# Mixture of experts: a third slot for expert weights, thirty blocks written out

## What is computed

```python
def expert_block(args):
    xb, e = args
    h = jax.nn.silu(xb @ w_gate[e]) * (xb @ w_up[e])
    return h @ w_down[e]

y_rows = lax.map(expert_block, (x_rows, block_e)).reshape(n_rows, d)
y = jax.ops.segment_sum(y_rows * row_gate[:, None], row_tok, num_segments=t + 1)[:t]
```

## Time and profile before

| | us |
|---|---|
| median of 3 runs | 4931.76 (4929.23 to 4942.64) |
| the profiled execution | 4922.4 |
| its span, first to last instruction | 4920.6 |
| experts of layer 0 / layer 1 within it | about 3115 to 3650 / 4291 to 4860 |
| TensorE busy | 3960.5 |
| VectorE / ScalarE / GpSimd busy | 1605.2 / 624.0 / 520.8 |
| moved by DMA | 708.19 MB, mean 144 GB/s |

### The profile page before, as it was taken

How to read it: one execution, slowest core, us unless ns; L and a number is a source line. 1 busy time by engine, 2 the same in 40 slices (tenths; PEclk the granted TensorE clock), 3 DMA queues, 4 the chain that set the end, 5 groups by cost and what they waited for, 6 DMA issues and landing times. The chain is left out here.

```text
span 4920.6 us, 53676 instructions
## 1 busy us (share of the span) xinstructions
PE 3960.5 (80%) x21959; PEld 2392.9 (49%) x21959; DVE 1605.2 (33%) x2927; ACT 624.0 (13%) x1247; POOL 520.8 (11%) x439
## 2 busy tenths in 40 slices
PE   4989978999898869998997548677757978587774
PEld 2578843444447734443476424344435756344442
DVE  6657733401384630002313651200021133310003
ACT  2211111000231220000111000000011022100000
POOL 1122310000101210001002311000010023100001
PEclk9999989999899989999997778799978997699997
DMA  3221215621220012221220011899972200499995
GB/s 121 69 74 50 105 47 189 204 81 60 61 69 10 2 67 83 69 90 47 83 77 1 0 60 58 332 401 402 405 278 80 74 1 1 170 394 399 401 408 234
DMA packets 243084, 708.19 MB, mean 144 GB/s; under 512 B 22140, under 2 KB 117812, under 8 KB 192084
## 3 DMA queue, kind: packets, MB, share of 16 engines
q1 hardware_dynamic: 223172, 662.03, 36.1%
q10 hardware_dynamic: 15120, 26.76, 1.5%
q0 software_dynamic: 4608, 16.78, 0.9%
HBM read 668.28 MB, written 37.24 MB: 143 GB/s over the span
## 5 line engine op out<-in xcount | busy, mean ns | idle before, releaser
L86 PE MATMUL ffn_in_ps<-ut,ffn_in_ring 128*128 128x512 f32 x1408 | 613.2, 596 | 25.5 <-DMA ffn_in_ring<-in_ffn_w_in 25.5
L2862 PE MATMUL experts_pg<-moe_wg,experts_xt 128*64 128x256 f32 x4224 | 515.1, 406 | 125.6 <-DMA moe_wg<-in_moe_w_up 104.9
L2862 PEld LDWEIGHTS experts_pg<-moe_wg,experts_xt 128*64 128x64 f32 x4224 | 326.3, 147 | 297.4 <-issue 145.5
L86 PEld LDWEIGHTS ffn_in_ps<-ut,ffn_in_ring 128*128 128x128 f32 x1408 | 266.6, 190 | 362.5 <-issue 336.2
L465 PE MATMUL ffn_out_y<-ffn_out_ring,ffn_h 128*128 128x512 f32 x704 | 308.4, 600 | 19.7 <-DMA ffn_out_ring<-in_ffn_w_out 19.7
L2877 PE MATMUL experts_py<-moe_wd,experts_ht 128*64 128x512 f32 x1056 | 266.6, 650 | 41.7 <-DVE experts_ht L2929 24.2
L86 PE MATMUL att_proj_ps<-att_proj_ring,ut 128*128 128x512 f32 x576 | 250.4, 598 | 16.3 <-DMA att_proj_ring<-in_attn_w_qkv 16.3
L2927 DVE TENSOR_TENSOR experts_h<-experts_hs,experts_pg 128x256 f32<-128x256 f32 x66 | 27.8, 422 | 628.1 <-ACT experts_hs L2896 628.1
L465 PEld LDWEIGHTS ffn_out_y<-ffn_out_ring,ffn_h 128*128 128x128 f32 x704 | 135.2, 193 | 190.1 <-issue 168.7
L86 PEld LDWEIGHTS att_proj_ps<-att_proj_ring,ut 128*128 128x128 f32 x576 | 177.7, 309 | 88.7 <-DMA att_proj_ring<-in_attn_w_qkv 16.7
L573 DVE TENSOR_TENSOR ffn_h<-ffn_in_act_out,ffn_in_ps 128x512 f32<-128x512 f32 x44 | 30.3, 688 | 531.9 <-ACT ffn_in_act_out L560 531.9
(11 more groups left out here) (632 smaller groups left out, 5478.1 us busy)
## 6 DMA issues: line engine op xcount, KB each, us to landing
moe_wg<-in_moe_w_gate SPq DMA_DIRECT2D x66, 2048.0 KB, 20.0
moe_wg<-in_moe_w_up SPq DMA_DIRECT2D x66, 2048.0 KB, 24.4
moe_wd<-in_moe_w_down SPq DMA_DIRECT2D x66, 2048.0 KB, 25.1
ffn_in_ring<-in_ffn_w_in SPq DMA_DIRECT2D x44, 1024.0 KB, 7.6
ffn_in_ada_ring<-in_ada_w SPq DMA_DIRECT2D x28, 1024.0 KB, 7.3
ffn_out_ring<-in_ffn_w_out SPq DMA_DIRECT2D x22, 1024.0 KB, 4.8
ssd_proj_ring<-in_ssd_w_in SPq DMA_DIRECT2D x20, 1024.0 KB, 5.3
att_proj_ring<-in_attn_w_qkv SPq DMA_DIRECT2D x9, 2048.0 KB, 7.9
```

The costliest lines, as they stand in the source:

```text
L86: last = nc.tensor.matmul(out, lhsT, rhs, start=(i == 0), stop=(i == len(pairs) - 1))
L2862: last = nc.tensor.matmul(pg[ch * SLOTS:(ch + 1) * SLOTS, b, side, 0:HH], xt[:, b, kk % MQ, kk // MQ, :], wg[:, b, side, kk, ch * HH:(ch + ...
```

## The change

There are three weight slots in place of two. The weights' buffers and semaphores move into a Stage of their own around routing and experts, so that its end adds a barrier; the outer one keeps its own. During routing three experts are loaded in place of two. In the experts' stage blocks 0 to 29 (`PLAIN`) are written out on every engine, with slot n mod 3 and the expert as a constant; blocks 30 and on run in the loop with slots 0 and 1. `load` on SP is split into `load_rows` and `load_weights`; the waits for rows are as before, those for the weights of a written-out block n are for gu_made and y_made of n - 2, that is block n - 3. All else is the same code, indented further.

```diff
+WSLOTS, PLAIN = 3, FIRST - 2
-        wg, wd = outer.sb("wg", [P, 2, 2, DK, HID]), outer.sb("wd", [P, 2, HK, D])
-        gu_in, d_in = ([outer.sem(f"{n}{b}") for b in range(2)] for n in ("gu_in", "d_in"))
+        weights = Stage(nc, f"moe_w{l}")
+        wg, wd = weights.sb("wg", [P, WSLOTS, 2, DK, HID]), weights.sb("wd", [P, WSLOTS, HK, D])
+        gu_in, d_in = ([weights.sem(f"{n}{b}") for b in range(WSLOTS)] for n in ("gu_in", "d_in"))
...
+        with weights:
...
-                    for b in range(2):
+                        for b in range(WSLOTS):
...
+                        def load_rows(i, b, first=False):
+                            r0 = sp.value_load(info[0:1, bass.ds(i + B, 1)], min_val=0, max_val=ASSIGN + SLOTS)
+                            if not first:
+                                sp.wait_ge(s["xt_made"], i - 1)
+                            for half in range(2):
+                                sp.dma_start(xg[half * SLOTS:(half + 1) * SLOTS, b, :],
+                                             x_rows[bass.ds(r0, SLOTS), half * HALF:(half + 1) * HALF]).then_inc(x_in[b], 16)
+
+                        def load_weights(e, w, before):
+                            sp.wait_ge(s["gu_made"], before)
+                            load_gate_up(sp, e, w)
+                            sp.wait_ge(s["y_made"], before)
+                            load_down(sp, e, w)
+
+                        for n in range(PLAIN):
+                            load_rows(n, n % 2, n < 2)
+                            if n >= WSLOTS:
+                                load_weights(slice(n, n + 1), n % WSLOTS, n - WSLOTS + 1)
+                        with sp.Fori(PLAIN // 2, more + 1) as it:
+                            for b in range(2):
+                                i = 2 * it + b
+                                e = sp.value_load(info[0:1, bass.ds(i, 1)], min_val=0, max_val=E - 1)
+                                load_rows(i, b)
+                                load_weights(bass.ds(e, 1), b, i - 1)
...
-                        pe.wait_ge(gu_in[b], 32 * it + 32)
+                            pe.wait_ge(gu_in[w], 32 * used + 32)
...
-                        pe.wait_ge(d_in[b], 16 * it + 16)
+                            pe.wait_ge(d_in[w], 16 * used + 16)
...
-                    one(0, 0, 0, True)
-
-                    one(1, 1, 0, True)
-                    with pe.Fori(1, more + 1) as it:
-                        for b in range(2):
-                            one(2 * it + b, b, it)
+                        for n in range(PLAIN):
+                            one(n, n % 2, n // 2, n % WSLOTS, n // WSLOTS, n < 2)
+                        with pe.Fori(PLAIN // 2, more + 1) as it:
+                            for b in range(2):
+                                one(2 * it + b, b, it, b, it - PLAIN // 2 + PLAIN // WSLOTS)
```

498 lines of the change are left out of this document (240 added, 258 removed).

## The result

The changed kernel takes 4966.84 us (median of 6 runs, 4954.52 to 4969.68), the kernel before 4934.08 beside it (6 runs, 4929.23 to 4942.64). The ratio is 1.0059, with a 95% interval of 1.0042 to 1.0075: some 29 us slower. The profiled execution of after took 4969.25 us (span 4967.3), against 4922.4 of before. The latter is a quick one: it lies under all six of these runs of before, and of the 58 runs of before beside the experiments only three lie under it. So where a stretch of its trace is set against that of another kernel, the difference is on the large side, by some 15 us over both layers: 4922.4 against medians of 4934 to 4940.

A forecast was written before the change was run, and what follows sets the result against it. TensorE bounds most of the kernel, DMA transfers the two layers' expert stretches. Per layer -16.9 + 7.5 + 10.8 + 1.2 = +2.6 us, +5 in both; from the 4931.8 median, 4937 was predicted, range 4917 to 4964.

The forecast's parts named there:

- The likeliest case, no change: Whole kernel: time between 4917 and 4947, within 0.3% (15 us) of before; chance 0.65.
- the 0.23 for slower: Whole kernel: chance 0.23 of a time over 4947, slower by more than 0.3%.
- Part 2: Experts' stage: the first loop load waits for block 1's transposes, so the DMA-bound stretch begins later: +7.5 us a layer.
- part 3: Routing: the third expert's load runs into the token scatter, so block 0 starts late: +10.8 us a layer, lower bound +6.
- Part 1: Experts' stage: one block's load fewer after routing, a whole block's pace: -16.9 us a layer, or -14.9 for weights alone.
- Part 4: Experts' stage: 28 more written-out blocks bring 19 code packets a layer, spread over the DMA engines: +1.2 us a layer.
- rival (a): Experts' stage: code packets crowd on few DMA engines, 4953 with two, 4972 with one; chance 0.20.
- the sum without code: Both layers: fewer loads, later stretch and scatter collision, -16.9 + 7.5 + 10.8 = +1.4 us a layer.
- Rival (c): Experts' stage: deeper prefetch lowers the pace below 16.9 us a block; at 16.4, -14 a layer, 4909; chance 0.06.
- Rival (b): Routing: the third load overlaps the scatter for free and block 0 isn't late: -8.2 us a layer, 4915; chance 0.06.

The follow-up runs named there:

- the third slot in loops: The changed kernel with only blocks 0 to 5 written out and 6 to 29 in a loop of six: 4955.35 us, 1.0033 of before.
- rows-first kernel: The changed kernel with blocks 6 to 29 in loops of six and the third expert loaded behind the rows of blocks 0 and 1: 4928.02 us, 0.9981 of before.
- weights-first one: The changed kernel with loops of six, third expert loaded late, and each block's gate and up loads issued before its rows: 4954.0 us, 1.0034 of before.

## Why the prediction was right or wrong

The range (4917 to 4964) holds the time: 1.0059 times the 4931.76 of the forecast's base is 4960.9, though the median measured beside it, 4966.84, lies just above. The likeliest case, no change, did not come; the 0.23 for slower did.

*Part 2 and part 3 came as drawn.* Block 0 is 10.5 and 11.0 us late (10.8 forecast), the first loop load goes out 18.0 and 18.1 us later (18.3). The work of scatter and weights simply adds up. Loading the third expert late gave 23 us back in one pair of kernels and 26 in the other; two layers at 10.8 are 21.6.

*Part 1 was too large, and a reason in it wrong.* From the first load once the experts run to block 9's gate/up before needs 133.1 and 135.1 us, the third slot in loops 121.0 and 120.1: one block fewer is worth 12.1 and 15.0 us there, not 16.9. The 2.0 us beyond the weights were put down to rows in and result out. The result is nearly free (0.1 to 0.2 us), and the rows are worth 1.4 of the stream.

*Part 4 is the step that failed.* The term was +1.2 a layer, from counting what the packets occupy on the latest engine. Written-out code alone costs 15 us by the medians, 7 to 8 a layer. The packets do spread over the engines, as I argued against rival (a); the premise that failed is that only occupied time counts. 14 packets from block 9 to 29 occupy 15 us in all, 1 us on each of 16 engines, and in the traces the 20 blocks take 0.4 to 0.5 us longer each, 8 to 10 us a layer. The premise nearly holds where no rows are in the stream (0.13 a block); with them, 8 KB pieces of the weights get slower. That in before two packets cost at most 1.3 each was read rightly, but 1.3 for each is nearly this: 19 of them at even 0.45 are 8.6. I took the end near zero where the row allowed 24.7.

The Trainium skill ("Runtime: NRT & Kernel Launch", Instruction fetch mechanics) calls the crossing of a 16 KB page mostly hidden. For TensorE that is what the rows show: it waits for the up weights, not for code. In a stream that fills all DMA engines the measured 15 us disagree: what is hidden from the engine that runs the code is not hidden from the transfers.

*Left out of the sum:* the third slot in loops costs 16 us where +2.8 was the sum without code. In the traces, beyond the sum, 4.3 and 2.2 us are lost by block 9, about 2 a layer from there to block 29, and 4 in the last blocks of layer 1 (block 29 to the last one 68.7 against 64.7 us, where no other kernel with its rows is under 68). Rival (c) did not come: a longer queue (27 to 32 us against 20) never gave a pace under 16.9, and in three layers of two kernels it went with 17.4 to 17.7 with almost no code packets.

The two halves add up: 15 for the code, 16 for the slot with its collision, 29 measured. That the time lies in the range is in part luck: its upper part was there for code packets that crowd on two engines, which they did not do. Rival (b) is out. Rival (a) foresaw the size (4953 to 4972) for another reason.

*Open.* Why a weight piece takes longer while another engine moves rows is not shown, and no run sets the spread by itself. Nor is it known what drives the engines apart in the rows-first kernel's layer 1, or what slows the weights-first one, where order and depth were changed together. Before has one trace, of a quick execution, so how its pace varies is open.

## What to carry to other kernels

Where all DMA engines are full, code that is fetched counts as traffic, here with eight to ten times its own time while 2 KB rows share the weights' queue, and with little without them: keep such a stretch in loops whose bodies are not fetched again (six blocks here), and write out only what lies before it. One more buffer in front of a full queue is worth what it fills of idle DMA time; look for that gap first, load into it and not beside other traffic that the next stage waits for, and go back to the shallow scheme afterwards. That is the version with 0.9954.

## What the runs showed of the hardware

- A code packet of 16 KB takes 1.1 us on one engine, yet 14 of them over 350 us went with 8 to 10 us of loss in a stream of 16 full engines with 2 KB rows in it, and with 2.6 us (0.13 a block) without the rows.
- An 8 KB weight piece took 369 to 411 ns on average while some engine moved 2 KB rows, 316 to 319 apart from them, 313 without any rows, at a busy share of 1.01 to 1.02 throughout.
- 16 DMA engines under a queue that never empties drift apart by up to 10.8 us within one layer (30 written out, no result writes); behind a single drain they stood at 1.4 to 2.6, and in before's layer 1 the spread fell from 3.8 to 0.9 without one. By the Trainium skill ("DMA: Bandwidth & Descriptors", Why a DMA increments its semaphore by 16 and not by 1) the engines finish independently and the semaphore counts them; the spread of the increments agrees, with 0.9 us at least.
- A loop body of six blocks, 1,032 TensorE instructions, was not fetched again: 2 code packets in 3268 to 3600, as against 14.
- 0.26 MB of rows in 2 KB pieces cost 1.4 us on the weights' own queue (0.6 at 424 GB/s), and 0.26 MB of results on the other queue 0.2 us at most.
